# Turning the gated products of the middle feed-forward steps: sixteen quarter transposes, or two whole ones and sixteen transfers

## The reference

```python
D_MODEL, SEQ, DEPTH, D_FF = 1024, 256, 2, 2816

def _rmsnorm(x, g):
    xf = x.astype(jnp.float32)
    y = xf * lax.rsqrt(jnp.mean(xf * xf, axis=-1, keepdims=True) + NORM_EPS)
    return (y * g.astype(jnp.float32)).astype(x.dtype)

def _swiglu(x, w_gate, w_up, w_down):
    return (jax.nn.silu(x @ w_gate) * (x @ w_up)) @ w_down

for l in range(DEPTH):
    x = x + 0.5 * _swiglu(_rmsnorm(x, ffn1_norm[l]), ffn1_w_gate[l], ffn1_w_up[l], ffn1_w_down[l])
    h = _rmsnorm(x, mix_norm[l])
    ...
    x = x + (g[:, :, 0] * y_a + g[:, :, 1] * y_b + g[:, :, 2] * y_c) @ w_out[l]
    x = x + 0.5 * _swiglu(_rmsnorm(x, ffn2_norm[l]), ffn2_w_gate[l], ffn2_w_up[l], ffn2_w_down[l])
return _rmsnorm(x, final_norm)
```

## Time and profile before

| | us |
|---|---|
| median of 3 runs | 1159.51 (1159.3 to 1159.74) |
| the profiled execution, its own time | 1159.99 |
| its span | 1158.2 |
| TensorE busy | 1148.3 (99%) |
| VectorE busy | 935.0 (81%) |
| ScalarE busy | 581.5 (50%) |
| GpSimd busy | 73.5 (6%) |

### The profile page before, as it was taken

One profiled execution on the slowest core, in us unless ns is written; L12 is line 12 of the kernel. 1 busy time (PEld: TensorE's weight loads), 2 busy tenths in 40 slices (PEclk: granted clock), 3 DMA queues, 4 the chain that ended last, 5 costly groups with the idle time before them and its releaser, 6 DMA issues.

```text
span 1158.2 us, 16246 instructions
## 1 busy us (share of the span) xinstructions
PE 1148.3 (99%) x5525; PEld 940.3 (81%) x5525; DVE 935.0 (81%) x1734; ACT 581.5 (50%) x757; POOL 73.5 (6%) x133
## 2 busy tenths in 40 slices
PE   9999999999999999999999999999999999999997
PEld 6888888887777888888888888888877788888886
DVE  6877887878977688778887887877898696888877
ACT  6444345456764464344454444454678635434433
POOL 2000000061000000000000000002510000000000
PEclk9999999999999999999999999999999999999999
DMA  8566555796325555655556556557943345655570
GB/s 289 189 214 216 179 187 163 238 252 199 135 74 182 182 161 202 217 192 183 195 177 202 180 178 218 182 183 216 281 155 108 144 142 182 219 181 168 197 236 37
DMA packets 151042, 215.21 MB, mean 186 GB/s; under 512 B 9184, under 2 KB 110160, under 8 KB 150992
## 3 DMA queue, kind: packets, MB, share of 16 engines
q1 hardware_dynamic: 148256, 209.64, 55.2%
q0 software_dynamic: 2048, 4.20, 1.6%
q10 hardware_dynamic: 688, 0.71, 0.2%
HBM read 209.28 MB, written 1.05 MB: 182 GB/s over the span
## 4 chain that ended last, share of the span: by engine, by line
PE 96%; DMA 2%; DVE 1%; issue 0%; SPq 0%; ACT 0%; POOLq 0%; POOL 0%; DVEq 0%
PE ps L1393 30%; PE ps L1395 29%; PE ps L1394 29%; PE ps L1607 2%; PE ps L1663 1%; PE ps L1635 1%; PE ps L1443 1%; DMA raw<-in_w_in_dram 1%; PE ps L1412 1%; DMA x<-in_x_dram 1%; DVE wlo L547 0%; PE ps L1694 0%; PE ps L1654 0%; SPq L508 0%; PE ps L1578 0%
## 5 line engine op out<-in xcount | busy, mean ns | idle before, releaser
L547 DVE TENSOR_TENSOR wlo<-raw,whi 128x2048 fp32r<-128x2048 f32 (+1 forms) x195 | 433.7, 2242 | 79.8 <-ACT whi L1138 57.7
L1138 ACT ACTIVATE whi<-raw 128x2048 fp32r<-128x2048 f32 (+1 forms) x195 | 366.1, 1879 | 257.6 <-PE ps L1395 251.7
L1393 PE MATMUL ps<-whi,ht_hi 128*128 128x512 f32 (+1 forms) x1192 | 465.5, 391 | 0.6 <-DVE wlo L547 0.6
L1395 PE MATMUL ps<-whi,ht_lo 128*128 128x512 f32 (+1 forms) x1192 | 460.8, 387 | 0.0
L1394 PE MATMUL ps<-wlo,ht_hi 128*128 128x512 f32 (+1 forms) x1192 | 460.3, 386 | 0.0
L1395 PEld LDWEIGHTS ps<-whi,ht_lo 128*128 128x128 f32 x1192 | 223.9, 188 | 46.0
L1393 PEld LDWEIGHTS ps<-whi,ht_hi 128*128 128x128 f32 x1192 | 224.0, 188 | 45.6 <-ACT whi L1138 1.1
L1394 PEld LDWEIGHTS ps<-wlo,ht_hi 128*128 128x128 f32 x1192 | 224.1, 188 | 43.7
L609 DVE STREAM_TRANSPOSE scr<-scr 32x128 f32<-32x128 f32 x688 | 208.4, 303 | 10.3
L1393 PE MATMUL ps<-whi,at_hi 128*128 128x512 f32 x304 | 118.5, 390 | 0.0
L1394 PE MATMUL ps<-wlo,at_hi 128*128 128x512 f32 x304 | 118.3, 389 | 0.0
(11 more groups left out here) (179 smaller groups left out, 787.4 us busy)
## 6 DMA issues: line engine op xcount, KB each, us to landing
raw<-in_ffn_w_down_dram SPq DMA_DIRECT2D x88, 512.0 KB, 4.8
raw<-in_w_in_dram SPq DMA_DIRECT2D x88, 512.0 KB, 4.6
raw<-in_ffn_w_gate_dram SPq DMA_DIRECT2D x85, 512.0 KB, 4.0
raw<-in_ffn_w_up_dram SPq DMA_DIRECT2D x85, 512.0 KB, 5.0
raw<-in_w_out_dram SPq DMA_DIRECT2D x16, 512.0 KB, 4.5
raw<-in_w_branch_c_dram SPq DMA_DIRECT2D x8, 512.0 KB, 4.2
qk<-gates POOLq DMA_DIRECT2D x32, 64.0 KB, 2.9
gates<-prob POOLq DMA_DIRECT2D x32, 64.0 KB, 6.3
```

The costliest lines, as they stand in the source:

```text
L547: nc.vector.tensor_tensor(wlo[:, n, 0:w], raw[:, n, 0:w], whi[:, n, 0:w].bitcast(F32), ALU.subtract).then_inc(lo_done, 1)
L1138: nc.scalar.activation(whi[:, n, 0:w], raw[:, n, 0:w], ACT.Copy).then_inc(hi_done, 1)
L1393: nc.tensor.matmul(o, xh, wh, start=start, stop=False)
L1395: return nc.tensor.matmul(o, xl, wh, start=False, stop=stop)
```

## The change

Steps 1 to 9 of every block (36 in all) are turned in another way. VectorE makes **two transposes over all 128 partitions** (128 x 256 elements each), which turn the 32 x 32 blocks inside their partition quarter, into `act_b`. **Sixteen transfers** of 32 x 128 elements (16 KB, 512 bytes per partition) then carry blocks between quarters from `act_b` to `act_x` (`cross_act`): five are issued by ScalarE, eleven by GpSimd, whose queue gets a loop over steps 1 to 9. Both lie in parts of `proj` that are unused in the feed-forward blocks. `act_round` waits for all sixteen (`act_crossed`, `act_crossed_rest`). Steps 0 and 10 keep the sixteen quarter transposes (`direct`), now into `act_x`. `silu` waits for the products of the step before (`act_done`), no longer for `act_rest`, since `sg` and the turned tile no longer share memory. The order of the blocks in `act_x` is by source quarter, so `act_round` and `act_rest` read and write it by blocks of 32 columns.

```diff
--- before.py
+++ after.py
@@ -153,8 +153,6 @@
         scr = sb("scr", [P, 4 * SEQ])
         sg = scr[:, 0:512].rearrange("p (t c) -> p t c", t=NT)
         act = scr[:, 512:1024].rearrange("p (t c) -> p t c", t=NT)
-        act_t = scr[:, 0:512].rearrange("p (j c) -> p j c", j=2)
         kvs = scr[:, :].rearrange("p (v g c) -> p v g c", v=2, g=2)
         gr = sb("gates", [P, NT * 3 * D])
         gate = gr[:, :].rearrange("p (b t c) -> p t b c", t=NT, b=3)
@@ -179,6 +177,9 @@
         w1 = [[v.rearrange("p (j c) -> p j c", j=8) for v in halves] for halves in
               ((w1_k[:, :], gr[:, 2048:3072]),
                (w1_v[:, :], p_t[:, 0:2, :].rearrange("p f c -> p (f c)")))]
+        pr_all = pr[:, :, :].rearrange("p t c -> p (t c)")
+        act_b = pr_all[:, 4096:4608]
+        act_x = pr_all[:, 4608:5120]
         pc_t = w1_k[:, 0:SEQ]
         sc_t = w1_k[:, SEQ:2 * SEQ]
         turned = [turned_1, prob_all[:, 1024:3072].rearrange("p (q c) -> p q c", q=4)]
@@ -270,6 +271,8 @@
         act_done = sem("act_done")
         at_ps = sem("at_ps")
         act_turned = sem("act_turned")
+        act_crossed = sem("act_crossed")
+        act_crossed_rest = sem("act_crossed_rest")
         ath = sem("ath")
         atl = sem("atl")
         proj_done = sem("proj_done")
@@ -448,15 +451,44 @@
         def step_bank(f, i):
             return (first_bank(f) if i == 0 else 2 if final(i) else 0) if isinstance(i, int) else 0
 
+        def direct(i):
+            return isinstance(i, int) and i in (0, NSTEP - 1)
+
+        def crossings(l, f, i):
+            return (l * 2 + f) * (NSTEP - 2) + i - 1
+
         def wait_turned(eng, l, f, i):
             r = l * 2 + f
             if by_pe(l, f, i):
                 eng.wait_ge(at_ps, 1)
+            elif direct(i):
+                eng.wait_ge(act_turned, r * NSTEP + i)
             else:
-                eng.wait_ge(act_turned, r * NSTEP + i)
+                eng.wait_ge(act_crossed, (crossings(l, f, i) + 1) * (16 * len(BY_ACT)))
+                eng.wait_ge(act_crossed_rest, (crossings(l, f, i) + 1) * (16 * len(BY_POOL)))
+
+        BY_ACT = [(3, 0), (3, 1), (3, 2), (3, 3), (2, 3)]
+        BY_POOL = [(a, q) for a in range(4) for q in range(4) if (a, q) not in BY_ACT]
+
+        def act_quarters(rows, b):
+            return act_b[rows, 128 * b:128 * b + 128], act_x[rows, 128 * b:128 * b + 128]
+
+        def cross_act(eng, l, f, i, blocks, done):
+
+            eng.wait_ge(act_turned, (l * 2 + f) * NSTEP + i)
+            apart(eng)
+            for a, q in blocks:
+                eng.dma_start(act_quarters(slice(32 * q, 32 * q + 32), a)[1],
+                              act_quarters(slice(32 * a, 32 * a + 32), q)[0]).then_inc(done, 16)
 
         def turned_product(l, f, i):
-            return ps[:, 2, :].rearrange("p (j c) -> p j c", j=2) if by_pe(l, f, i) else act_t
+            src = ps[:, 2, :] if by_pe(l, f, i) else act_x
+            if by_pe(l, f, i):
+                return src.rearrange("p (e a c) -> p e a c", e=4, a=4)
+            return src.rearrange("p (a e c) -> p e a c", e=4, a=4)
+
+        def by_blocks(part):
+            return part.rearrange("p j c -> p (j c)").rearrange("p (e a c) -> p e a c", e=4, a=4)
 
         def act_parts(i):
 
@@ -602,17 +634,23 @@
 
             def turn_product(l, f, i):
                 dve.wait_ge(act_done, (l * 2 + f) * (2 * NSTEP) + i * 2 + 2)
-                src = act.rearrange("p t (j c) -> p t j c", j=2)
-                dst = act_t.rearrange("p j (t c) -> p t j c", t=NT)
-                for a in range(0, P, 32):
-                    for q in range(0, P, 32):
-                        ins = nc.vector.transpose(dst[q:q + 32, :, :, a:a + 32], src[a:a + 32, :, :, q:q + 32])
+                if direct(i):
+                    src = act.rearrange("p t (j c) -> p t j c", j=2)
+                    dst = act_x.rearrange("p (a j t c) -> p a t j c", a=4, j=2, t=NT)
+                    for a in range(4):
+                        for q in range(0, P, 32):
+                            ins = nc.vector.transpose(dst[q:q + 32, a], src[32 * a:32 * a + 32, :, :, q:q + 32])
+                else:
+                    dst = act_b.rearrange("p (q j t c) -> p t q j c", q=4, j=2, t=NT)
+                    for t in range(NT):
+                        ins = nc.vector.transpose(dst[:, t], act[:, t, :].rearrange("p (j q c) -> p q j c", j=2, q=4))
                 ins.then_inc(act_turned, 1)
 
             def act_rest(l, f, i):
                 dve.wait_ge(ath, (l * 2 + f) * NSTEP + i + 1)
                 hi, lo = act_parts(i)
-                nc.vector.tensor_tensor(lo, turned_product(l, f, i), hi.bitcast(F32), ALU.subtract).then_inc(atl, 1)
+                nc.vector.tensor_tensor(by_blocks(lo), turned_product(l, f, i), by_blocks(hi).bitcast(F32),
+                                        ALU.subtract).then_inc(atl, 1)
 
             def ffn(l, f):
                 n, s0 = 2 * f, f * (FFN_SLABS + MIX_SLABS)
@@ -1102,8 +1140,13 @@
                         src = turned[n][32 * a:32 * a + 32, q, :].rearrange("p (e c) -> p e c", e=4 * NT)
                         pool.dma_start(dst.rearrange("p g t c b -> p (g t) (c b)"), src).then_inc(crossed[n], 16)
 
+            def ffn(l, f):
+                norm(l * 3 + 2 * f)
+                with pool.Fori(1, NSTEP - 1) as i:
+                    cross_act(pool, l, f, i, BY_POOL, act_crossed_rest)
+
             for l in range(DEPTH):
-                norm(l * 3)
+                ffn(l, 0)
                 norm(l * 3 + 1)
                 cross(l, 0)
                 pool.wait_ge(crossed[0], (l + 1) * 256)
@@ -1115,7 +1158,7 @@
                         apart(pool)
                         gv = gate[:, t, w // 2, (w % 2) * 512:(w % 2 + 1) * 512]
                         nc.gpsimd.tensor_scalar(gv, gv, 0.5, 0.5, ALU.mult, ALU.add).then_inc(gate_ready, 1)
-                norm(l * 3 + 2)
+                ffn(l, 1)
 
 
             for t in range(NT):
@@ -1174,7 +1217,7 @@
                 for t in range(NT):
                     if not first:
 
-                        eng.wait_ge(atl, r * NSTEP + i)
+                        eng.wait_ge(act_done, r * (2 * NSTEP) + i * 2)
                     nc.scalar.activation(sg[:, t, :], ps[:, t + step_bank(f, i), 0:FSTEP], ACT.Silu,
                                          scale=rstd[:, t:t + 1]).then_inc(silu_done, 1)
 
@@ -1183,7 +1226,7 @@
 
                 if not isinstance(i, int):
                     wait_used(eng, l, (i, f * (FFN_SLABS + MIX_SLABS) + 1))
-                nc.scalar.activation(act_parts(i)[0], turned_product(l, f, i), ACT.Copy).then_inc(ath, 1)
+                nc.scalar.activation(by_blocks(act_parts(i)[0]), turned_product(l, f, i), ACT.Copy).then_inc(ath, 1)
 
             def ffn(l, f):
                 n, s0 = 2 * f, f * (FFN_SLABS + MIX_SLABS)
@@ -1215,11 +1258,13 @@
                     convert(l, (i, s0 + 2))
                     silu(l, f, i, False)
                     convert(l, (i, s0 + 3))
+                    cross_act(eng, l, f, i, BY_ACT, act_crossed)
                     convert(l, (i, s0 + 4))
                     act_round(l, f, i)
                 convert(l, s0 + 3 * last - 1)
                 silu(l, f, last - 1, False)
                 convert(l, s0 + 3 * last)
+                cross_act(eng, l, f, last - 1, BY_ACT, act_crossed)
                 act_round(l, f, last - 1)
                 convert(l, s0 + 3 * last + 1)
                 silu(l, f, last, False)
```

## The result

| | before | after |
|---|---|---|
| median, us | 1159.55 (4 runs) | 1186.49 (4 runs, 1185.37 to 1189.83) |
| the profiled execution | 1159.99 | 1185.69 |
| its span | 1158.2 | 1183.9 |

The ratio is 1.0237, with a 95% interval of 1.0216 to 1.0259: slower by 27 us, where 12.8 were forecast.

A forecast was written before the change was run, and what follows sets the result against it. TensorE, busy 99% of the span, was taken as the bound; VectorE's relief counted 0, the loop 0, block-end waits four times 3.2 us, 12.8: 1172.8 against the profiled 1159.99, so median 1172.3, range 1166 to 1184.

The forecast's parts named there:

- VectorE's 150 us: Shorter transposes in 36 steps save VectorE 4.28 us each, 154 in all, none on TensorE's path: worth 0.
- The loop was called hidden: In the loop the rest ends at some 124.5, wanted at 128.3: worth 0 while the landing stays under 3.7 us.
- The Trainium skill's trap: Some VectorE operations lock GpSimd out of writing descriptors; the trace doesn't show it for those used here; no size given.
- ten starts: In each crossing, GpSimd's issues start every 0.59 us: 5.89 us to the start of the eleventh.
- The circle of that step: In the loop, crossing to rounding, ScalarE's and VectorE's conversions and next product: 15.1 us against a step of 16.32.
- the rival of the overrun: In the loop, landings over 3.7 us or issues of 0.71 or more make TensorE wait: 1180 to 1222; chance 0.13.
- Both signs of being wrong: Issues much less than 0.58 us, or landings beside the loads over 3.7 us.
- ends of the blocks: Ahead of down(10), TensorE waits 3.2 us in each of four blocks: 12.8 us.
- lower clock after a wait: After a block-end wait the clock drops to 1.2 GHz for one slab: 5.4 us per block, 22 in all; chance 0.07.
- landing of the last: In each crossing, the last GpSimd transfer lands 2.5 us after its start, with 5.3 kept as the bound.
- had queued up behind each other: Reading of earlier 64 KB transfers: the last five's landings of 4.9 to 5.6 us came from queueing; new ones taken at 2.5.
- Slab 31 itself is in time: At the block's end, slab 31 is done at 176.9, wanted 5.4 us before 182.72.

The follow-up runs named there:

- run 5: The changed kernel with all sixteen transfers per step left out and the rounding reading `act_b`: 1159.58 us, ratio 0.9996 to the kernel before.
- run 1: The changed kernel with step 9 turned as before by sixteen quarter transposes, crossings in steps 1 to 8 alone: 1164.92 us, ratio 1.0038.
- run 2: The changed kernel with SyncE's load of the first slab after a block held until step 9's crossing has landed: 1176.36 us, ratio 1.013.
- Run 12: The changed kernel with 44 small useless matmuls on TensorE between down(9) and down(10): 1180.05 us, ratio 1.0173.
- Run 3: The kernel before with eleven idle 16 KB GpSimd transfers in each of 36 steps, which only GpSimd waits for: 1165.05 us, ratio 1.0043.
- run 4: The kernel before with twelve further transposes into unused memory ahead of step 9's own, no transfers added: 1172.34 us, ratio 1.0106.

## Why the prediction was right and wrong

**Right: which engine bounds, and what the removed part is worth.** VectorE's 150 us were put at 0, and run 5 shows 0. The loop was called hidden: 32 crossings cost 0.7 us (run 1). GpSimd issued eleven in 5.37 us, one every 0.49, while VectorE converted. The Trainium skill's trap (SBUF: State Buffer, VectorE's operations that lock GpSimd out) doesn't show here, as was weighed.

**Right: the place and the mechanism.** Four waits ahead of down(10), released by `ht_lo`, because the conversion of slab 31, silu(10) and the product of step 10 are queued behind a rounding that is late. The row from rounding to rest, forecast at 13.6 us (172.07 to 185.65), took 172.92 to 186.54: 13.6.

**Right by luck: the loop.** It was hidden because two errors cancelled. The rounding of the step in the earlier trace rows starts at 124.05 for a forecast 123.1: its crossing took 11.2 us, with a landing of 4.0 where 3.7 was the bound, and with ten starts in 4.9 us where 5.9 were forecast. The circle of that step comes to 15.9 us by these, against 16.32, with 0.4 to spare instead of 1.2. With the landing as measured and the starts as forecast it would come to 16.9, an estimate from the same rows, and the rival of the overrun would have been the case. Both signs of being wrong that the prediction named, issues well under 0.58 and landings over 3.7, did appear.

**Wrong: the size, and so the range.** 27 us, where 12.8 were forecast and 24.5 (1184) were the end of the range. The profiled execution took 1185.69, 12.9 more than the 1172.8 forecast for it. By the table of places above:

| place | in the sum | measured |
|---|---|---|
| ends of the blocks | 12.8 | 15.8 |
| lower clock after a wait | 0, a rival | 3.5 |
| waits in the loop | 0, "hidden" | 1.7 |
| behind the last output transfer | no term | 5.3 |
| small differences | no term | -0.6 |

So the crossing's own terms missed by 3.0, and what the sum had at nothing by the rest. Without the tail of 5.3 us the median would lie inside the range, near 1181. The crossing, step by step, first block:

| term | forecast | measured |
|---|---|---|
| product and transposes | 1.68 | 1.68 |
| to GpSimd's first transfer | 0.32 | 0.59 |
| ten starts | 5.89 | 4.87 |
| landing of the last | 2.5 | 4.0 (blocks 2 and 3: 4.9, 4.7; block 4: 2.6) |
| in all | 10.4 | 11.2 |

- The term of the crossing that failed is the landing, "the new ones are a quarter of the size at the same pace, so I take 2.5". With the load held they land in 1.6 to 2.7 (run 2). What I left out is that VectorE, 3.7 us earlier at slab 30, lets SyncE's next load go 3.7 us earlier, into the last transfers. I priced the relief of VectorE at 0 and didn't ask what it would trigger. Run 2 takes the collision away and gets 10 us back. The Trainium skill's fixed 2.0 us for a transfer (DMA: Bandwidth & Descriptors, anatomy of one DMA) agrees with the case without a load beside, 1.6 to 2.7, and not with 3.7 to 4.9 beside one; by it the forecast would have been lower still.
- The reading behind that term, that the late landings in the earlier trace rows "had queued up behind each other", had a rival in the same trace. The transfer of `cross` issued at 236.08 landed in 2.8 us, the next one, at 236.65, in 4.7, at the same pace of issues; and at 236.71 SyncE starts two loads:

```profile
DMA to landing us min/median/max: 2.8/2.8/2.8
...
DMA to landing us min/median/max: 4.7/4.7/4.7
...
236.71 0.91 SPq L1808 DMA_DIRECT2D raw<-in_w_in_dram  x2
```

  Two loads started at 233.14 and 233.53 had left the landings at 2.4 to 2.8, so this was a hint and not a proof. In run 2 eleven in a row land in 1.6 to 1.7 each in the first block: no queue there.

- "Slab 31 itself is in time", by 0.4 us, was too thin a margin: with the later landing TensorE also waited ahead of down(9), 2.9 us in three blocks.
- The issues were mis-sized the other way, 0.49 in place of 0.59, which is 1.0 us per block. Without that error the forecast would have been lower still, 1168.
- The clock was held a rival, with 0.07 and 22 us. It did fall, after two of four waits in the profiled execution, and cost 1.7 us each time, not 5.4. Run 12 shows that TensorE's idleness brings it: with matmuls in the wait the clock stays. The Trainium skill's rule that an idle TensorE loses its clock (TensorE: Matmul & The Clock Gate) agrees with the trace (0.50 after two waits of 2.98 us), and should have been a term of the sum once the sum had a wait of 3 us in it.
- The tail (5.3 us), the largest single part of the miss, and GpSimd's pause in the loop (1.7 us) were no case at all. Nothing in the profile before shows them; there GpSimd issues 64 transfers. Run 3 makes both pauses and tail without the change.

Summed by what the runs isolate: the crossing of step 9 costs 21.6 us of 27 (run 1 against the changed kernel); 10 of these are the moved load (run 2), waits and lower clock taken together. The remaining 5 are the tail, 4.4 us in run 1, and one wait in the loop; what sets the tail's size stays open.

## What to carry to other kernels

When a change relieves an engine off the critical path, list what that engine releases, loads above all, and put the new start times beside the transfers that the change adds: here a load 3.7 us earlier made the last transfers, on which everything waited, land 2.2 to 2.4 us later. Look, too, at what else starts where a duration in the trace jumps, before calling it a queue. Look at the seams of a loop apart from its body: 32 steps hid a crossing of 11 us, and the step before last, with 1 us of slack, paid for it, so turning that one step as before removed most of the loss. A forecast wait of a few us on TensorE should carry a term for the clock, and small matmuls without use in the wait can keep it.

## What the runs showed of the hardware that was not expected

- A transfer of 16 KB between partitions, issued by GpSimd, takes 0.49 us to issue (64 KB ones: 0.58). The last of eleven lands 1.6 to 2.7 us after its start with no load beside it, 4.0 to 4.9 when two loads of 512 KB have started 2 to 3 us before (changed kernel and run 2, ends of the first three blocks).
- Waits of 2.98 us on TensorE lowered the granted clock in two of three cases, waits of 2.25 and, in run 2, 2.48 didn't, but one of 2.10 did there (0.83 in 760 to 770 us), and one of 1.92 in run 4 (0.83 in 170 to 180), of four such. The same wait may or may not cost the clock.
- GpSimd pauses in a row of transfers, waiting for nothing visible: 4.9 to 6.0 us after the 259th in the changed kernel and in runs 2, 3 and 12, which have eleven a step, up to 15.5 with eight a step. Such kernels also end 1.6 to 6.2 us later after their last output transfer. Only having the transfers brings it; the rule behind the sizes stays open.
